# Two transformer blocks on one core: the head of the program reordered, the last norm's roots moved off GpSimd, the output stored by half rows

## What is computed

```python
h = rmsnorm(x, mix_pre_g)
proj = h @ w_in          # q, k, v, two gates, two halves of a gated MLP, forget logits
...
x = x + rmsnorm(merged @ w_out, mix_post_g)
h = rmsnorm(x, ffn_pre_g)
x = x + rmsnorm(swiglu(h, w_gate, w_up, w_down), ffn_post_g)
```

## Time and profile before

| | us |
|---|---|
| median of 3 runs | 1699.59 (1698.79 to 1699.95) |
| the profiled execution, its span | 1699.3 |
| PE busy | 1639.2 (96%) |
| DVE, ACT, POOL busy | 684.9, 525.3, 509.9 |
| chain that ended last, share of PE | 92% |
| mean granted clock of PE | 0.982 |

### The profile page before, as it was taken

The page is one execution under the profiler, slowest core; times in us unless marked ns, Lnnn a source line. Parts: engine busy times, 40 slices in busy tenths (PEclk is TensorE's granted clock), DMA queues, the critical chain, the costliest instruction groups (busy, mean ns, idle before and its releaser), DMA issues.

```text
span 1699.3 us, 19149 instructions
## 1 busy us (share of the span) xinstructions
PE 1639.2 (96%) x7330; PEld 1309.6 (77%) x7330; DVE 684.9 (40%) x795; ACT 525.3 (31%) x725; POOL 509.9 (30%) x449
## 2 busy tenths in 40 slices
PE   5999999999989999999899999999999999999997
PEld 3878777788868888888776665688887788888886
DVE  3223444347543333322344654554434433333223
ACT  5222322232342222222334453222224422222121
POOL 2760001300178000087201686168102880000000
PEclk9999999999989999999999999999999899999999
DMA  6533111231535333344220232134323353333331
GB/s 166 179 115 99 50 50 50 75 99 60 164 100 148 99 99 99 99 148 159 83 81 25 74 113 86 50 100 149 99 99 99 115 147 92 92 98 99 102 109 50
DMA packets 187687, 170.76 MB, mean 100 GB/s; under 512 B 20592, under 2 KB 159856, under 8 KB 187632
## 3 DMA queue, kind: packets, MB, share of 16 engines
q1 hardware_dynamic: 179568, 144.84, 28.1%
q0 software_dynamic: 8064, 25.20, 4.7%
HBM read 167.91 MB, written 2.10 MB: 100 GB/s over the span
## 4 chain that ended last, share of the span: by engine, by line
PE 92%; DVE 2%; SPq 2%; ACT 1%; POOL 1%; issue 1%; DMA 0%; DVEq 0%; POOLq 0%; ACTq 0%
PE bank L1360 28%; PE bank L1361 27%; PE bank L1362 27%; SPq L497 1%; PE bank L1646 1%; PE bank L1503 1%; PE bank L1519 1%; PE bank L1595 1%; PE bank L1501 1%; PE bank L1571 1%; POOL inv_rms L587 1%; PE bank L1511 1%; PE bank L1502 0%; PE bank L1636 0%; PE bank L1467 0%
## 5 line engine op out<-in xcount | busy, mean ns | idle before, releaser
L1360 PE MATMUL bank<-h_hi,w_hi 128*128 128x512 f32 x1376 | 555.5, 404 | 12.6 <-DVE w_lo L968 6.3
L1361 PE MATMUL bank<-h_lo,w_hi 128*128 128x512 f32 x1376 | 540.1, 393 | 0.0
L1362 PE MATMUL bank<-h_hi,w_lo 128*128 128x512 f32 x1376 | 540.0, 392 | 0.0
L968 DVE TENSOR_TENSOR w_lo<-raw,w_hi 128x2048 fp32r<-128x2048 f32 (+1 forms) x146 | 311.1, 2132 | 357.2 <-ACT w_hi L691 357.0
L691 ACT CAST w_hi<-raw 128x2048 fp32r<-128x2048 f32 (+1 forms) x146 | 250.9, 1718 | 258.5 <-PE bank L1362 254.4
L1360 PEld LDWEIGHTS bank<-h_hi,w_hi 128*128 128x128 f32 x1376 | 261.0, 190 | 80.6 <-issue 20.3
L1362 PEld LDWEIGHTS bank<-h_hi,w_lo 128*128 128x128 f32 x1376 | 260.8, 190 | 55.4
L1361 PEld LDWEIGHTS bank<-h_lo,w_hi 128*128 128x128 f32 x1376 | 261.3, 190 | 53.5 <-issue 1.9
L616 POOL TENSOR_SCALAR mod_raw<-mod_raw,c_silu 128x512 f32<-128x512 f32 x96 | 182.2, 1898 | 37.8 <-DMA mod_raw<-in_mod_w 33.9
L586 POOL TENSOR_SCALAR sq_y<-sq_y 128x1 f32<-128x1 f32 x16 | 8.0, 501 | 513.6 <-ACT y_down L697 324.8
L619 POOL TENSOR_TENSOR mod_acc<-mod_acc,mod_raw 128x512 f32<-128x512 f32 x96 | 145.4, 1514 | 8.2
(11 more groups left out here) (276 smaller groups left out, 1760.6 us busy)
## 6 DMA issues: line engine op xcount, KB each, us to landing
raw<-in_w_in SPq DMA_DIRECT2D x102, 512.0 KB, 4.5
mod_raw<-in_mod_w POOLq DMA_DIRECT2D x96, 256.0 KB, 3.1
raw<-in_w_ffn_in SPq DMA_DIRECT2D x44, 512.0 KB, 4.8
raw<-in_w_gate SPq DMA_DIRECT2D x22, 512.0 KB, 3.9
raw<-in_w_up SPq DMA_DIRECT2D x22, 512.0 KB, 5.2
raw<-in_w_down SPq DMA_DIRECT2D x20, 512.0 KB, 4.0
raw<-in_w_ffn_out SPq DMA_DIRECT2D x20, 512.0 KB, 4.2
raw<-in_w_out SPq DMA_DIRECT2D x8, 512.0 KB, 4.4
```

Of the source, the lines that this page charges most:

```text
L968: ins = dve.tensor_tensor(w_lo[s][:, cols], raw[s][:, cols], w_hi[s][:, cols].bitcast(F32), ALU.subtract)
L1360: pe.matmul(o, st_hi, mv_hi, start=first, stop=False)
L1361: pe.matmul(o, st_hi, mv_lo, start=False, stop=False)
L1362: return pe.matmul(o, st_lo, mv_hi, start=False, stop=last)
```

## The change

SP loads x and gain_1 ahead of unit 0, and unit 0's halves get separate semaphores (`raw_first` for the first), so that ACT and DVE split it in two steps (`hi_first`, `lo_first`), and PE starts on its first four k-tiles after the first. ACT no longer multiplies x by the root; DVE does both halves. POOL makes the identity, then x's roots, then the masks. What needs the small loads is moved: on ACT behind the take of unit 1, on DVE ahead of the k units. In the last norm ACT takes the square root, with a table load of its own, and DVE refines it with five operations on 128x1 in the place of POOL's power. Each row tile of the output is stored in two halves.

```diff
 def lay_out_stream():
-    raw = [0, 0]
+    raw = [-16, 0]
...
         ACT_STEPS = ["q0 q1 s0 q2 n0 s1 q3 n1 s2 s3 n2 n3", "q0 q1 s0 q2 s1 q3 s2 n0 n1 s3 n2 n3",
-                     "q0 q1 s0 q2 n0 s1 q3 n1 s2 s3 n2 n3", "q0 q1 q2 q3"]
+                     "q0 q1 s0 q2 n0 s1 q3 n1 s2 s3 n2 n3", "q0 e0 q1 e1 q2 e2 q3 e3"]
...
-            load_f(n_q, w_in, Q_COL)
             for t in range(NT):
                 sp.dma_start(x_in[:, t, :], x_v[:, t, :]).then_inc(x_loaded[t], 16)
             with nc.allow_non_contiguous_dma(reason="a few hundred scalars, once"):
                 sp.dma_start(gain_1[:], column("mix_pre_g")).then_inc(gain_1_in, 16)
+            r = ktiles(raw[0], 8, 256)
+            sp.dma_start(r[:, 0:4, :], w_in[:, 0:4, Q_COL:Q_COL + 256]).then_inc(raw_first, 16)
+            load(n_q, r[:, 4:8, :], w_in[:, 4:8, Q_COL:Q_COL + 256])
             load_f(n_q + 1, w_in, Q_COL + 256)
             load_small()
...
             for t in range(NT):
-                sp.wait_ge(x_added, 8 * 3 + 2 * t + 2)
-                sp.dma_start(out_v[t], x_res[:, t, :]).then_inc(stored, 16)
-            sp.wait_ge(stored, 16 * NT)
+                for half, cols in enumerate(HALVES):
+                    sp.wait_ge(x_added, 8 * 3 + 2 * t + half + 1)
+                    sp.dma_start(out_v[t][:, cols], x_res[:, t, cols]).then_inc(stored, 16)
+            sp.wait_ge(stored, 32 * NT)
...
+            then(gp.memset(power[:], -0.5))
+            triangle(ident_r, 1.0, 0.0, -1, 1, ALU.is_equal).then_inc(consts, 1)
+            gp.wait_ge(consts, 1)
+            for t in range(NT):
+                gp.wait_ge(x_squared, 2 * t + 2)
+                root(sq_x, t, x_root)
...
-            for t in range(NT):
-                gp.wait_ge(x_squared, 2 * t + 2)
-                root(sq_x, t, x_root)
             gp.wait_ge(c_ready, 1)
             mod_pair(0)
...
             mod_pair(5)
-            post_norm(3)
...
                 for j in range(units):
                     split(n0 + j + 1)
+                if k == 3:
+                    act.preload_act_table(ACT.Sqrt)
                 for t in range(NT):
                     square_bank(0, t)
...
+                    elif what == "e":
+                        act.wait_ge(y_squared, 8 * k + NT + t + 1)
+                        act.wait_ge(sq_shifted, 1)
+                        act.activation(rms_y[:, t:t + 1], sq_y[:, NT + t:NT + t + 1], ACT.Sqrt,
+                                       bias=sq_y[:, t:t + 1]).then_inc(y_root, 1)
...
-            split(0)
             for t in range(NT):
                 act.wait_ge(x_loaded[t], 16)
                 for half, cols in enumerate(HALVES):
                     square(xn_1[:, t, cols], x_in[:, t, cols], sq_x[:, NT * half + t:NT * half + t + 1]).then_inc(x_squared, 1)
-                if t > 0:
-                    norm_rows(0, x_in, xn_1, t - 1)
-            norm_rows(0, x_in, xn_1, NT - 1)
+            act.wait_ge(raw_first, 16)
+            act.copy(w_hi[0][:, 0:1024], raw[0][:, 0:1024]).then_inc(hi_first, 1)
+            split(0, part=1)
             act.wait_ge(gain_1_in, 16)
             hi_parts(0, gain_1, None)
             split(n_q + 1)
-
-            act.wait_ge(small_in, 16 * SMALL)
-            act.copy(wf_hi[:], wf[:]).then_inc(wf_split, 1)
...
             for j in range(4):
                 if j > 0:
                     split(n_q + j + 1)
                 take(n_q + j, 0, q_t[:, 2 * j, :], STILL, ACT.Copy, float(P) ** -0.5)
+                if j == 1:
+                    act.wait_ge(small_in, 16 * SMALL)
+                    act.copy(wf_hi[:], wf[:]).then_inc(wf_split, 1)
+                    act.copy(wf2_hi[:], wf2[:]).then_inc(wf_split, 1)
+                    act.activation(c_silu[:], c_col[:], ACT.Silu).then_inc(c_ready, 1)
+                    act.preload_act_table_set("natural_log_exp_and_others")
+                    then(act.activation(a_neg[0:HEADS, :], a_log[0:HEADS, :], ACT.Exp))
...
+            def refine_root(t):
+                total, step, inv = root_tmp[:, 0:1], root_tmp[:, 1:2], inv_rms[:, t:t + 1]
+                dve.wait_ge(sq_shifted, 1)
+                then(dve.tensor_tensor(total, sq_y[:, t:t + 1], sq_y[:, NT + t:NT + t + 1], ALU.add))
+                then(dve.reciprocal(inv, rms_y[:, t:t + 1]))
+                then(dve.scalar_tensor_tensor(step, inv, inv, total, ALU.mult, ALU.mult))
+                then(dve.tensor_scalar(step, step, -0.5, 1.5, ALU.mult, ALU.add))
+                then(dve.tensor_tensor(inv, inv, step, ALU.mult))
...
                 for t in range(NT):
                     gain_bank(0, t)
+                if k == 3:
+                    dve.tensor_scalar(sq_y[:, 0:NT], sq_y[:, 0:NT], EPS, None, ALU.add).then_inc(sq_shifted, 1)
...
                         dve.wait_ge(y_root, NT * k + t + 1)
+                        if k == 3:
+                            refine_root(t)
...
-            split(0)
             for t in range(NT):
-                norm_rows(0, x_in, xn_1, t)
+                dve.wait_ge(x_root, t + 1)
+                for cols, ready in zip(HALVES, (xn_a_ready, xn_b_ready)):
+                    dve.tensor_scalar(xn_1[:, t, cols], x_in[:, t, cols], inv_rms[:, t:t + 1], None, ALU.mult).then_inc(ready, 1)
+            dve.wait_ge(hi_first, 1)
+            dve.tensor_tensor(w_lo[0][:, 0:1024], raw[0][:, 0:1024], w_hi[0][:, 0:1024].bitcast(F32), ALU.subtract).then_inc(lo_first, 1)
             dve.wait_ge(gain_1_in, 16)
-            lo_parts(0, gain_1, None)
-            dve.wait_ge(small_in, 16 * SMALL)
-            dve.wait_ge(wf_split, 2)
...
+            lo_parts(0, gain_1, None, after_two=lambda: split(0, part=1))
             for n0, dst in ((n_q, q_t), (n_k, k_t)):
+                if n0 == n_k:
+                    dve.wait_ge(small_in, 16 * SMALL)
+                    dve.wait_ge(wf_split, 2)
...
-                wait(pe, lo_done, n + 1)
+                if n == 0:
+                    pe.wait_ge(lo_first, 1)
+                else:
+                    wait(pe, lo_done, n + 1)
...
                 for k in range(KD):
+                    if n == 0 and k == 4:
+                        wait(pe, lo_done, 1)
...
             pe.wait_ge(wf_split, 3)
+            pe.wait_ge(consts, 2)
             narrow(wf_hi, wf_lo)
```

More of the change, by code:

```diff
@@ L267, in build @@
         inv_rms = small("inv_rms", NT)
+        rms_y = small("rms_y", NT)
+        root_tmp = small("root_tmp", 2)
         neg_max = small("neg_max", 2)
@@ L282, in build @@
         raw_in = sems("raw_in0", "raw_in1")
+        raw_first, hi_first, lo_first = sems("raw_first", "hi_first", "lo_first")
         hi_done, lo_done = sems("hi_done", "lo_done")
@@ L562, in _, with triangle, root @@
             then = chain.then
+            def triangle(t, keep, fill, step, mult, op):
+                then(gp.memset(mod_acc[:, 0, 0:P], keep))
+                return gp.affine_select(out=t[:], in_=mod_acc[:, 0, 0:P], compare_op=op, fill=fill, base=0,
+                                        pattern=[[step, P]], channel_multiplier=mult)
+            def root(sq, t, ready):
+                total = sq[:, t:t + 1]
+                then(gp.tensor_scalar(total, total, sq[:, NT + t:NT + t + 1], EPS, ALU.add, ALU.add))
+                gp.tensor_tensor(inv_rms[:, t:t + 1], total, power[:], ALU.pow).then_inc(ready, 1)
+            then(gp.memset(power[:], -0.5))
[4 more added lines that the diff above has]
+                root(sq_x, t, x_root)
             for t, keep, fill, step, mult, op in (
-                    (ident_r, 1.0, 0.0, -1, 1, ALU.is_equal),
                     (mask_qk, 0.0, MASKED, -1, 1, ALU.is_ge),
@@ L572, in _ @@
                     (neg_suffix, -1.0, 0.0, -1, 1, ALU.is_ge)):
-                then(gp.memset(mod_acc[:, 0, 0:P], keep))
-                then(gp.affine_select(out=t[:], in_=mod_acc[:, 0, 0:P], compare_op=op, fill=fill, base=0,
-                                      pattern=[[step, P]], channel_multiplier=mult))
+                then(triangle(t, keep, fill, step, mult, op))
             then(gp.tensor_tensor(head_sel[:], ident[0:64, 0:HEADS], ident[0:64, 32:32 + HEADS], ALU.add))
@@ L578, in _ @@
             then(gp.tensor_scalar(neg_ones[:], ones[:], -1.0, None, ALU.mult))
[L579 to L587, removed]
+            gp.tensor_scalar(zeros_st[:], ones[:, 0:1], 0.0, None, ALU.mult).then_inc(consts, 1)
+            gp.wait_ge(consts, 2)
             def post_norm(k):
@@ L793, in _ @@
             split(n_q + 1)
-            act.wait_ge(small_in, 16 * SMALL)
-            act.copy(wf_hi[:], wf[:]).then_inc(wf_split, 1)
-            act.copy(wf2_hi[:], wf2[:]).then_inc(wf_split, 1)
-            act.activation(c_silu[:], c_col[:], ACT.Silu).then_inc(c_ready, 1)
-            act.preload_act_table_set("natural_log_exp_and_others")
-            then(act.activation(a_neg[0:HEADS, :], a_log[0:HEADS, :], ACT.Exp))
             for j in range(4):
@@ L978, in norm_rows, with lo_parts @@
```

(14 more changed lines are left out.)

6 lines of the change are left out of this document (2 added, 4 removed).

## The result

The changed kernel takes 1689.76 us in the median of 4 runs (1688.46 to 1690.82); the kernel before, run beside it, takes 1699.19 (1697.88 to 1699.95). The ratio is 0.9946, with a 95% interval of 0.9933 to 0.9959: faster by 9.4 us, where the prediction said 6.0. The profiled execution's span is 1689.1 us against 1699.3, 10.2 less.

What follows compares the result with a forecast made beforehand. PE was taken as the bound, busy 96% of the span, so only its holes could be won. Head -8.8, clock +1.8 and tail +1.0 (+1.6 - 0.6) sum to -6.0 us: 1693.6 us, range 1688 to 1697.

Steps and rivals of the forecast that it cites:

- rival (a): Head: small loads clear sooner, unit 2's weights land 3.7 us sooner, PE never stops; 1688.1 us; chance 0.13.
- main case: Whole kernel: head -7.0 us, tail +1.0, with a 3.7 us hole before unit 2; 1693.6 us; chance 0.72.
- Small loads waited for later: Head: waits moved later; PE's 6.33 us hole before unit 1 goes; ACT's later block costs nothing.
- x ahead of the weights: Head: first matmul at 14.7 us, 4.4 earlier; unit 1 ends at 40.8; buys only 0.6 us at unit 2.
- I keep 40.3: Head: second load of unit 2's weights still lands at 40.3 us, 1 us either way; hole of 3.7 us.
- rival (b): Head: small loads clear later, SP stalls at more issues, each 2.9 us; two give 1699.4, three 1702.3; chance 0.07.
- The clock term: Behind the hole before unit 2: the clock falls and costs 1.8 us, bounds 0 and 2.6.
- The roots on DVE: Tail: five small DVE operations add 1.0 us a tile, gains 3.05 us apart, last x_res 1.6 us later.
- rival (c): Last norm: Square and Sqrt alternate on ACT and each switch loads a table; 1696.1 us; chance 0.03.
- The half-row stores: Tail: last store carries 256 KB instead of 512, saving 0.6 us, bounds 0 and 1.3.
- the base of the sum: Tail: end taken as set by the last store, so +1.6 and -0.6 us count there, sum +1.0.
- POOL's pair goes: Last norm: POOL's root operations are dropped; ACT's Sqrt instead, 0.2 us a tile, costs nothing.

Runs made afterwards that it cites:

- e3: Kernel before with only the waits for the small loads, and the work behind them, moved later on ACT and DVE: ratio to before 0.9947.
- e1: Kernel before with all head edits (x ahead of the weights, small-load waits moved, POOL's order), old tail: ratio to before 0.9968.
- e6: Kernel before with the small-load waits moved and the change's tail, x left behind unit 0's weights: 1686.28 us, ratio to before 0.9920.
- e4: Changed kernel plus a POOL memset at its end, after ACT's last squares, that nobody reads: 1692.27 us, ratio to before 0.9963.
- e7: Changed kernel with the output stored by whole rows again, four stores of 512 KB: ratio to before 0.9941.
- e8: Changed kernel with only the reciprocal left on DVE in the last norm, Newton step and its sum left out: ratio to before 0.9931.
- e2: Kernel before with only the tail edits (last norm's roots on ACT and DVE, half-row stores), old head: ratio to before 0.9979.
- e10: Kernel before with only the output stored by half rows: ratio to before 1.0001.
- e5: Changed kernel with unit 2's weights loaded after the first 11 small loads, unit 3's behind the rest: 1681.4 us, ratio to before 0.9898.
- e12: Changed kernel with unit 2's weights after the first 11 small loads and no Newton step in the last norm: 1676.55 us, ratio to before 0.9887.

## Why the prediction was right in its sign and off in its size

By the profiled executions the span fell by 10.2 us: 4.8 up to unit 4's start (75.07 to 70.32), 2.0 in the middle, 3.4 behind the last matmul. The prediction had 7.0, 0 and -1.0. Its head was 2.2 too good, its tail 4.4 too bad, and 2.0 came from nowhere in it; the errors partly cancel, and that the measured 1689.76 lies inside the stated range owes something to luck. By the time alone rival (a), 1688.1, would look nearer than the main case, 1693.6; the trace shows the main case's hole, and (a) did not happen. (The 0.3 us that the sum adds to a span are the distance of two different executions, not the 1.7 of a run to its own span; they cancel in the difference.)

**Small loads waited for later: right.** PE's 6.3 us hole is gone, ACT's later block makes nobody wait, and e3 shows that this edit alone carries the head.

**x ahead of the weights: mechanism right, sizes near.** First matmul 15.21 against a forecast 14.7, end of unit 1 at 41.24 against 40.8, both 0.5 late. That x first would buy hardly anything as long as unit 2's weights don't move was in the text ("only 0.6 of it"). It was still too kind: e1 against e3 shows a loss of 1.2 us (x first with all that comes with it, the split of unit 0 and POOL's order too), since without x first the hole is 0.36 us (1.38 in e6), and no clock is lost.

**"I keep 40.3" failed.** The second half of unit 2 landed at 42.2, 1.9 late and outside the 1 us that I allowed. The reading behind it (the queue is still at the small loads, so their end sets the landing) stands; the claim that this end stays does not. Two things moved it. The first is SP's issue of the second half, at 33.34 instead of 31.73 (+1.6). SP gets to the small loads at 9.38 instead of 8.06, but most of that is made up at once: c_col's issue takes 0.51 us now and took 3.23, wf's takes 2.85 and took 1.00, and behind wf2 the lag is 0.44. The rest comes late, above all at the first short_w (1.64 us instead of 0.55, at 28.57). Four issues take over 2 us, as before, so this is not rival (b), which had more of them stall. It isn't the new order as such either: e1, with the same head, issues the second half at 32.04, and over its five profiles (after, e1, e4, e7, e8) the landing lies between 40.8 and 42.2. The second is the time from issue to landing, 8.8 against 8.6 here. In e3 and e6, with x where it was, it is 9.9, and the second half lands at 41.1 and 41.5. In all of these unit 3's loads follow directly, where they used to wait until 40.6; that this makes the difference is argued, not tested, and it doesn't say why 8.8 stand beside 9.9. So the landing was kept 0.5 to 1.9 us too early for every head with the waits moved, and the hole was 5.25 us and not 3.7.

**The clock term: right, in part by luck.** It fell, and cost 2.1 us against a forecast 1.8. The forecast was for a hole of 3.7 us; whether the clock falls in one that short, no run shows (in e1, e7 and e8 it fell 5.0 us behind PE's stop). The price is no constant either: much the same hole (5.2 to 5.7 us) cost 1.6 in e1, 1.8 in e4, 3.0 in e7 and e8.

**The roots on DVE: right to a tenth.** Gains 3.08 apart (forecast 3.05), x_res 1.7 later behind the last matmul (forecast 1.6). Sqrt took 0.30 us, not 0.2, under cover. No table load stands between squares and roots, only one at 1612.0. There rival (c) falls. The Trainium skill (ScalarE: Activation LUTs, Table sets: the hidden batching unit) wants calls batched by set, and its table of sets names no function beside sqrt; by this trace Square runs on under Sqrt's set, four times in turn, at its old 0.60 us.

**The half-row stores: right, 0.6 us (2.6 against 2.0; e7).** The Trainium skill (DMA: Bandwidth & Descriptors, Anatomy of one DMA — SWDGE (gpsimd) path) gives a transfer that GpSimd issues a fixed part of about 2.0 us and its bytes by 436 GB/s. An estimate by it is 2.6 and 3.2 us; these stores, which SP issues, took 2.0 and 2.6, so the difference of 0.6 us for 256 KB agrees and the fixed part does not (it is 1.4 us here).

**What failed at the tail is the base of the sum.** The text added +1.6 and -0.6 to an end that it took to be set by the last store. In the kernel before it was not: x_res and its store had 5 us of slack under POOL's drain. Removing POOL's roots takes away 5.0 us (1694.28 to 1699.27), and only then do the two terms count: 1.7 - 0.6 - 4.6 = -3.5 (the 4.6 is 5.0 less the 0.4 that remain behind the last landing), against 3.4 measured. The row was in the trace; x_res ending at 1691.6 and landing 2.6 later leaves 5 us to the span's end unexplained, and I did not ask what fills them. In the prediction's words, "POOL's pair goes" was costed only as instructions, and not as the last thing that POOL does. e2, e4 and e10 show each side of it.

**The middle.** Its 2.0 us belong to no step. Fourteen profiled executions of the same middle lie between 1605.7 and 1613.3, and the kernel before had the longest. That execution holds two waits of PE, 2.1 us for sp_lo and 1.2 for g_ssd, that none of the other 13 shows. In e10, the same kernel but for its stores, the middle is 1611.2 long, as in the changed kernel (1611.3). So the 2.0 us are put down to that one profile. In the interval's terms the change gives 7 to 11.4 us; head and tail by the profiles give 8.2.

## What to carry to other kernels

Close the account at both ends before pricing an edit: from the last matmul to the last landing to the end of the span, naming what each piece waits for, the closing instructions of every queue too. An engine whose closing drain is long (POOL's 8.9 us here) should not be given the last small operation. An earlier start is worth nothing until the next operand is earlier too, and can be worth less than nothing when the hole that it opens costs clock; move the loads (e5) in the same step as the start.

## What was not expected of the hardware

- POOL's drain at the end of its program takes 8.9 us, in every profile: rows of 8883 ns where nothing stands ahead of it, and of 8999 to 9502 where they cover a last memset or root. The drain rows of DVE (1.4 us), ACT (0.3 to 0.7) and PE's weight queue (4.0) are long only by what they cover: each ends within 0.1 us of its engine's last operation. SP's takes 7 ns. Why POOL's is so long was not tried; that it drives 96 DMAs of its own is a guess.
- The granted clock fell at differing times behind PE's stop at the end of unit 1: 2.0 us (e4), 2.6 (the changed kernel) and 5.0 (e1, e7, e8), and stayed at 1.2 GHz for 3.4 or 6.8 us.
- In the middle of the kernel low stretches of 3.4 to 13.7 us lie at much the same places of nearly every execution (near 320, 465, 840, 890, 1090 and 1310 us); their lengths differ, and one or the other is missing at times (e5, e7 and e12 have none near 1090, e6 none near 320; the kernel before has one at 1024 in the place of that near 890). They add up to 41.0 us in e5, e6, e7 and e12, whose middles are four of the five shortest (1605.7 to 1609.4), and to 44 to 55 in the others. They explain the spread of the middle only in part: e6's middle is 3.5 us longer than e5's at the same sum.
